# A decoder kernel whose logarithm and exponential share one table load, and whose weight blocks come in two transfers each

## What is computed

```python
def stick_breaking_attention(q, k, v):          # A[t,s] = beta[t,s] * prod_{s<j<t} (1 - beta[t,j])
    ...
    mask = s_idx < t_idx
    log_keep = jnp.where(mask, jax.nn.log_sigmoid(-logits), 0.0)
    later = lax.cumsum(log_keep, axis=log_keep.ndim - 1, reverse=True) - log_keep
    log_a = jax.nn.log_sigmoid(logits) + later
    a = jnp.where(mask, jnp.exp(log_a), 0.0)
    ...

def s5_mixer(h, ...):
    ...
    g = jax.nn.gelu(y).astype(h.dtype)
    val, gate = jnp.split(g @ w_glu, 2, axis=-1)
    return val * jax.nn.sigmoid(gate)
```

## Time and profile before

| | us |
|---|---|
| median of 3 runs | 1056.37 (1052.62 to 1057.84) |
| the profiled execution | 1056.6 |
| its span, from the first to the last instruction | 1054.8 |
| PE busy | 931.1 (88%) |
| DVE busy | 574.7 (54%) |
| ACT busy | 461.0 (44%) |
| POOL busy | 125.4 (12%) |
| DMA | 163.93 MB, mean 155 GB/s |

### The profile page before, as it was taken

How to read it: one execution, slowest core, us unless ns; L and a number is a source line. 1 busy time by engine, 2 the same in 40 slices (tenths; PEclk the granted TensorE clock), 3 DMA queues, 4 the chain that set the end, 5 groups by cost and what they waited for, 6 DMA issues and landing times.

```text
span 1054.8 us, 11941 instructions
## 1 busy us (share of the span) xinstructions
PE 931.1 (88%) x4951; PEld 766.0 (73%) x4951; DVE 574.7 (54%) x751; ACT 461.0 (44%) x568; POOL 125.4 (12%) x71
## 2 busy tenths in 40 slices
PE   4999999989999999897699999984445999999998
PEld 3887777777787886786588888774335877888886
DVE  4654555561244766666576899632620555545453
ACT  4534555458934636244244444422212544444441
POOL 1000002020000020202844444000002000000000
PEclk9999999996999998698899999995765999999999
DMA  8525644441014554004447566643997454455441
GB/s 322 184 88 192 239 160 160 163 156 42 1 68 156 165 199 163 3 2 160 149 165 255 201 230 217 218 162 40 102 149 278 140 211 157 162 185 214 160 160 40
DMA packets 72736, 163.93 MB, mean 155 GB/s; under 512 B 2041, under 2 KB 12874, under 8 KB 72170
## 3 DMA queue, kind: packets, MB, share of 16 engines
q1 hardware_dynamic: 68304, 149.03, 43.4%
q10 hardware_dynamic: 2234, 6.69, 2.1%
q0 software_dynamic: 2144, 7.43, 2.0%
HBM read 150.57 MB, written 11.53 MB: 154 GB/s over the span
## 4 chain that ended last, share of the span: by engine, by line
PE 42%; DVE 6%; DMA 3%; SPq 3%; ACT 2%; issue 1%; POOL 0%; POOLq 0%; ACTq 0%
PE bank L560 13%; PE bank L562 12%; PE bank L561 12%; DVE wlo L1333 3%; SPq L506 3%; DMA ring<-in_w_glu 2%; PE bank L814 1%; DMA aux<-h 1%; ACT whi L1003 1%; DMA ring<-scratch_readout 1%; PE bank L553 1%; DVE aux L1726 1%; PE bank L925 1%; PE bank L895 1%; PE bank L859 0%
## 5 line engine op out<-in xcount | busy, mean ns | idle before, releaser
L1333 DVE TENSOR_TENSOR wlo<-ring,whi 128x2048 fp32r<-128x2048 f32 (+1 forms) x122 | 307.5, 2528 | 248.3 <-ACT whi L1003 248.3
L1003 ACT ACTIVATE whi<-ring 128x2048 fp32r<-128x2048 f32 (+1 forms) x124 | 236.2, 1910 | 343.9 <-PE bank L562 241.3
L560 PE MATMUL bank<-whi,hT_hi 128*128 128x512 f32 (+1 forms) x736 | 292.4, 397 | 21.8 <-DVE hT_lo L1324 10.3
L561 PE MATMUL bank<-wlo,hT_hi 128*128 128x512 f32 (+1 forms) x736 | 289.7, 394 | 0.0
L562 PE MATMUL bank<-whi,hT_lo 128*128 128x512 f32 (+1 forms) x736 | 289.4, 393 | 0.0
L560 PEld LDWEIGHTS bank<-whi,hT_hi 128*128 128x128 f32 x736 | 140.5, 191 | 52.1 <-DVE hT_lo L1324 8.7
L562 PEld LDWEIGHTS bank<-whi,hT_lo 128*128 128x128 f32 x736 | 140.5, 191 | 29.1
L561 PEld LDWEIGHTS bank<-wlo,hT_hi 128*128 128x128 f32 x736 | 140.6, 191 | 28.1
L560 PE MATMUL bank<-whi,hidT_hi 128*128 128x512 f32 x256 | 100.7, 393 | 2.1 <-DVE hidT_lo L1719 2.1
L562 PE MATMUL bank<-whi,hidT_lo 128*128 128x512 f32 x256 | 99.8, 390 | 0.0
L561 PE MATMUL bank<-wlo,hidT_hi 128*128 128x512 f32 x256 | 99.6, 389 | 0.0
(11 more groups left out here) (232 smaller groups left out, 1044.2 us busy)
## 6 DMA issues: line engine op xcount, KB each, us to landing
ring<-in_w_ff SPq DMA_DIRECT2D x32, 2048.0 KB, 7.7
ring<-in_ple_gate_w SPq DMA_DIRECT2D x4, 2048.0 KB, 7.9
ring<-in_w_kv SPq DMA_DIRECT2D x4, 2048.0 KB, 8.0
ring<-in_b_w_in SPq DMA_DIRECT2D x4, 2048.0 KB, 8.5
ring<-in_w_glu SPq DMA_DIRECT2D x4, 2048.0 KB, 9.0
ring<-in_a_w_in SPq DMA_DIRECT2D x3, 2048.0 KB, 9.2
ring<-in_w_in SPq DMA_DIRECT2D x3, 2048.0 KB, 8.1
ring<-in_a_w_out SPq DMA_DIRECT2D x2, 2048.0 KB, 8.0
```

What stands on the lines that cost most here:

```text
L560: pe.matmul(bank_cols, high[:, at[0], at[1]], w_high, start=first, stop=False)
L561: pe.matmul(bank_cols, high[:, at[0], at[1]], w_low, start=False, stop=False)
L1003: act.activation(whi[at], ring[:, slot[name], cols], ACT.Copy).then_inc(high_made, 1)
L1333: dve.tensor_tensor(wlo[at], ring[:, slot[name], cols], whi[at], ALU.subtract).then_inc(low_made, 1)
```

## The change

It has two parts.

1. ACT loads a set by name, `natural_log_exp_and_others`, ahead of the stick-breaking loop, and finds both functions in it.
2. Every split block comes in two transfers of half a block, each with a semaphore of its own (`block_landed[slot][half]`), and ACT's `fill(g)` waits for its own half alone. SP waits ahead of each half: for the first, that the first half of the low part of block n - 2 is made (both halves where the two blocks differ in size), for the second, that both are. Where block n - 2 isn't a split one, both halves wait for its product, as before. Blocks that aren't split come in whole.

```diff
+    landed, arrived = {}, [[0, 0] for _ in range(RING)]
+    for name, parts, _ in blocks:
+        counts = arrived[slot[name]]
+        for half in range(2 if name in order else 1):
+            counts[half] += 16 if name in order else 16 * len(parts)
+            landed[name, half] = counts[half]
...
-        block_landed = [sem(f"block_landed{i}") for i in range(RING)]
+        block_landed = [[sem(f"block_landed{i}{half}") for half in "ab"] for i in range(RING)]
...
+                if name in order:
+
+                    (_, src), = parts
+                    k, width = src.shape[1] // 2, src.shape[2]
+                    for half in range(2):
+                        if n >= RING:
+                            before, _, reader = blocks[n - RING]
+                            if before in order:
+                                whole = size[before] != size[name] or half
+                                sp.wait_ge(low_made, 2 * order[before] + (2 if whole else 1))
+                            else:
+                                sp.wait_ge(pe_done, done(reader))
+                        dst = ring[:, slot[name], half * k * width:(half + 1) * k * width]
+                        sp.dma_start(dst.rearrange("p (k n) -> p k n", k=k), src[:, half * k:(half + 1) * k])\
+                            .then_inc(block_landed[slot[name]][half], 16)
+                    continue
...
             def fill(g):
 
                 name, cols, at = half_of(g)
-                if g:
-                    act.wait_ge(block_landed[slot[name]], landed[name])
-                else:
-                    act.wait_ge(first_landed, 16)
+                act.wait_ge(block_landed[slot[name]][g % 2], landed[name, g % 2])
...
             turned_out("q", [(qT, "q_norm", True)])
+            act.preload_act_table_set("natural_log_exp_and_others")
             for j in range(NH // 2 + 1):
```

More of the change, by code:

```diff
@@ L319, in program @@
     slot = {name: n % RING for n, (name, _, _) in enumerate(blocks)}
[L320 to L323, removed]
     done = u.done
@@ L399, in program @@
                                                       for n in ("inject", "readout", "taps"))
-        high_made, low_made, high_turned, inv_ready, gelu_high, relu_ready, first_used, exps_ready, first_landed = (
+        high_made, low_made, high_turned, inv_ready, gelu_high, relu_ready, first_used, exps_ready = (
             sem(n) for n in ("high_made", "low_made", "high_turned", "inv_ready", "gelu_high", "relu_ready",
-                             "first_used", "exps_ready", "first_landed"))
+                             "first_used", "exps_ready"))
         def half_of(g):
@@ L477, in _ @@
             sp.dma_start(ring[:, 0, 0:BLK // 2].rearrange("p (k n) -> p k n", k=KC // 2), first[:, 0:KC // 2])\
-                .then_inc(first_landed, 16)
+                .then_inc(block_landed[0][0], 16)
             sp.wait_ge(x_landed, 16)
             sp.dma_start(ring[:, 0, BLK // 2:BLK].rearrange("p (k n) -> p k n", k=KC // 2), first[:, KC // 2:KC])\
-                .then_inc(block_landed[0], 16)
+                .then_inc(block_landed[0][1], 16)
             for n, (name, parts, _) in enumerate(blocks):
@@ L506, in _ @@
                         sp.dma_start(ring[GI * j:GI * j + GI, slot[name], :].rearrange("p (g n) -> p g n", n=P), src)\
-                            .then_inc(block_landed[slot[name]], 16)
+                            .then_inc(block_landed[slot[name]][0], 16)
                     continue
@@ L513, in _ @@
                         dst = dst.rearrange("p (k n) -> p k n", k=src.shape[1])
-                    sp.dma_start(dst, src).then_inc(block_landed[slot[name]], 16)
+                    sp.dma_start(dst, src).then_inc(block_landed[slot[name]][0], 16)
             for t in range(NT):
@@ L540, in weights_here @@
             def weights_here(name):
-                pe.wait_ge(block_landed[slot[name]], landed[name])
+                pe.wait_ge(block_landed[slot[name]][0], landed[name, 0])
             def turn(stage, src, units=range(4), width=P, chunks=8, ready=None):
```

## The result

| | before | after |
|---|---|---|
| median, us | 1056.97 (1052.62 to 1057.84) | 1036.41 (1035.9 to 1044.95) |
| profiled execution, us | 1056.6 | 1036.74 |
| span, us | 1054.8 | 1034.9 |
| PE busy, us | 931.1 | 919.7 |
| ACT busy, us | 461.0 | 443.1 |

The ratio is 0.9839 (95% interval 0.9805 to 0.9872), a gain of 20.6 us between the medians. The 14 runs of the three sets go from 1035.2 to 1045.0 us with a median of 1039.0, so the gain is nearer to 18 than to 21 us. Both medians, 1036.4 and 1039.0, lie outside the forecast range. The forecast was 1046.2 us with a range of 1041 to 1051.5: right in sign and too small. All medians and ranges are of runs in the fast state; one run of `tables` took 1374.06 us at a mean clock of 0.642, where its others had 0.93, and is left out.

The account below looks back on a forecast made before the run. PE was taken to bound the large-product stages, leaving gains only in the stick-breaking loop, bound by PE once ACT's loads go, and the S5 stage. 7.1 + 2.7 + 0.6 = 10.4 us off 1056.6 gives 1046.2 us, range 1041 to 1051.5.

Parts of the forecast that it names:

- loop, low stretch as long as before: Stick-breaking loop: one table load gains 7.1 us, from 3.8 of PE's waits, 3.2 of low-clock spells and 0.1.
- PE's waits for low parts: Between 300 and 345: PE's one wait for a low part, 0.6 us, should go.
- `readout` 1: S5 stage: it is issued and lands 2.7 us earlier, cutting PE's wait from 3.2 to 0.5 us; gain 2.7.
- the first stretch at the low clock: Loop's start, 20.48 us long: the change doesn't touch the wait ahead, PE bounds already, only 0.1 us gained.
- The only rival on the clock that I priced for that stretch: Loop: low clock stays, each further step costs 4.5 us, 1077 us with all six; chance of three or more 0.04.
- it waits only before the last sums: Loop's last step, which has no logits: about 0.5 us of PE's wait stays; elsewhere the round trip is hidden.
- the spells of 3.4 us: Loop: two low-clock spells, at 279.02 and 292.67, go with the waits preceding them; gain 3.2 us.
- The step was forecast at 5.43 us: Loop: each step is cut from 6.15 to at most 5.43 us, the 0.72 that PE waits for `sps`.
- the first rival: Loop: the clock dips all the same, so the total gain is 7.2 us and the time 1049.4; chance 0.2.
- The rival in which PE isn't the bound: Loop: PE's busy time hides slack, saving 15 us there at the most, time 1038; chance 0.05.
- land apart and in order: S5 stage: the first half of ("val", 0) lands 2.7 us ahead of the whole block, bounds 2.3 and 3.3.
- 27 us of PE's waits for the taps: S5 stage: PE's 27 us of waiting for the taps don't change, as they come in ahead of the block.

Follow-up runs that it names:

- the three sets: The changed kernel timed three times, unaltered, the second and third beside other kernels on their chips: ratios 0.9839, 0.9835 and 0.9843 to the kernel before.
- tables: The kernel before with the one table load alone, transfers whole: 1045.82 us, ratio 0.9901.
- val0_dve: The changed kernel with the two low parts of block ("val", 0) made by VectorE in place of GpSimd: 1037.42 us, ratio 0.9816.
- again: The changed kernel once more, unaltered: 1038.59 us, ratio 0.9835.
- again_2: The changed kernel a third time, unaltered: 1040.49 us, ratio 0.9843.
- tables_again: The kernel before with the one table load alone, once more on another chip: 1045.86 us, ratio 0.9898.
- act_extra: The changed kernel with an unread 128x512 copy on ACT behind each final exponential, 16 in the loop: 1040.64 us, ratio 0.9854.
- filled_before: The kernel before with seven unused 128x512 products on PE in its wait for the turned q ahead of the loop: 1058.56 us, ratio 1.0007.
- halves: The changed kernel without the table line, so half transfers alone: 1050.69 us, ratio 0.9939.
- val0_only: The changed kernel with only block ("val", 0) and the very first split block in halves, all others whole: 1043.9 us, ratio 0.9883.
- filled4_dve: The changed kernel with four unused products in PE's wait ahead of the loop and ("val", 0)'s low parts on VectorE: 1034.12 us, ratio 0.9795.

## Why the prediction was wrong in size

The forecast gain was 10.4 us: 7.1 for the loop, 2.7 for the S5 stage and 0.6 near 342. The two profiles differ by 19.9 us, 9.5 more. Of these, 6.0 are in the loop (13.1 against 7.1), 2.2 ahead of it, 0.3 between loop and S5 stage, and 1.0 in the S5 stage. Term by term:

| term | forecast | shown |
|---|---|---|
| loop, low stretch as long as before | 7.1 | 8.6 (`tables`, `val0_dve`) |
| loop, the stretch shorter | 0 | 4.5 (after, `again`, `again_2`) |
| PE's waits for low parts | 0.6 | 0.7 near 122 and 0.9 near 342 |
| `readout` 1 | 2.7 | about 1.4, of which 1.0 is its own wait and 0.4 that for `readout` 0 |

**The step that failed** is the one on the first stretch at the low clock: in it "PE bounds already, and next to nothing (0.1 us) is gained". That took its 20.48 us as given, like a piece of the code. It isn't: `tables` and `tables_again` are the same code and had 20.5 and 10.2 us; after, `again`, `again_2` and `act_extra` had 10.2, and `val0_dve`, whose code up to there is theirs, 20.5. With the long one the loop takes 51.20 us, with the short one 46.66: each microsecond at the low clock costs 0.44 us, since PE now bounds. Without any stretch it takes 42.57, 8.6 us less than with the long one; in the kernel before, with ACT as the bound, the same removal gave 2.9 us (`filled_before`, with one short spell more). The only rival on the clock that I priced for that stretch was that it lasts longer, 4.5 us per step. The same price should have stood on the other side of the forecast: one step less gives 1041.7, and two give 1037. With this term at 4.5 instead of 0.1 the forecast would have been 1041.8. Of the eight profiled loops with one table load and no fillers six had 10.2 us and two 20.5, so the shorter one is the more frequent there; why can't be told from these traces. The one run of before that was profiled had 20.48, and whether its other runs do is open. For that reason the 4.5 us are shown between profiles only; that the medians of the runs lie apart by it isn't shown.

**The rest of the loop was sized too small**, by 1.5 us. 0.9 of them are the stretch that in `tables` began 1.05 us ahead of the first logits, 0.15 ahead in before; the remainder lies behind the stretch. The mechanism held: PE is the bound, it waits only before the last sums (0.30 us, forecast 0.5), and the spells of 3.4 us went with the waits. The step was forecast at 5.43 us, the 6.15 less the wait of 0.72. The end of the last logits, from which that wait is counted, is hidden where the sums follow at once: they then start 2.04 us behind the first logits, not 2.19, and the step is 5.23. Of the first rival (the clock dips all the same), nothing was seen: no profile with the one table load has a dip behind the first stretch. The rival in which PE isn't the bound had a time (1038) close to the result, but that is luck, not its mechanism: `act_extra` keeps ACT busy for 7.5 us more, and the loop grows by 0.8.

On the Trainium skill's price for a switch of table sets (ScalarE: Activation LUTs, What ACT_TABLE_LOAD costs), 2.66 us with a drain: ACT was busy for 50.36 us in the loop of `halves` and 30.14 in that of `tables`, a difference of 20.2 us for 17 loads, or 1.2 us for each; a drain of 1.38 us isn't in it, nor is it idle time, of which ACT's loads had 0.1 us in front of them. The measurement decides for 1.28 us.

**The halves.** That they land apart and in order was right: 2.60 us apart, forecast 2.7. The halves of `("val", 0)` bring the issue of `readout` 1 from 11.0 us behind the block's last byte (before, `tables`, `tables_again`, `filled_before`) to 8.4 (the eight halved kernels with GpSimd): 2.6 us, as forecast. What was wrong is that all of this would reach PE. The transfer of `readout` 1 takes 7.3 to 7.7 us in those four and 8.3 to 9.0 in those eight, and PE's wait for it falls only from 3.4 on the mean to 2.4; another 0.4 us comes from `readout` 0, which PE gets earlier in the seven with all blocks in halves (a wait of 7.4 us; 7.9 in `val0_only`). The prediction let a transfer start earlier and keep its length. Its 27 us of PE's waits for the taps were also misread, 15.58 + 13.47 = 29.1 in before; no term uses them. It named only one wait of PE for a low part and missed the one at 122, which it had not looked for.

The stage shows the same when the taps, which scatter by 8.6 us, are taken out of it (us; the taps from their first issue to their last landing):

| | S5 stage less taps | mean |
|---|---|---|
| the four with whole blocks | 50.6 to 51.9 | 51.3 |
| the eight with halves, low parts on GpSimd | 49.3 to 50.5 | 49.8 |
| the two with low parts on VectorE | 46.3 and 47.2 | 46.7 |

So the halves alone are worth 1.5 us here, and the faster engine behind them another 3.0.

**What belongs to chance.** Of the 19.9 us between the two profiles, about 1.6 are a low spell at 186.9 in before that is absent in after, and also in `tables` and `halves`, and some 2.2 are the taps, whose transfers took 42.95 us in before and 40.71 in after. In the other kernels, which issue the same taps, they took from 39.1 to 47.7 us. The attributable terms (loop, the two waits for low parts, the S5 stage) come to 8.6 + 1.6 + 1.4 = 11.6 us with the long stretch and 16.1 with the short one. The measured gain of 18 us is a little more than that, and the 2 us between aren't assigned.

**The range.** It held the sides of the mechanisms that I had named, but 2 us of spread for the runs was too little: the runs of the kernel before alone go from 1051.4 to 1062.4 on one chip. The bound of the range at 1041 was also drawn without any case below it but one of 0.05.

## What to carry to other kernels

When an edit makes another engine the bound, first price what that engine's own changing state costs, in both directions: here 10 us more or less at TensorE's low clock became worth 4.5 us as soon as PE bounded. Functions that alternate in a loop should come from one table set, and what that is worth is read from the waits of the engine behind it, not from the loads removed (20.2 us off ACT gave 8.6 to 14.3). A transfer that is issued earlier moves next to another one: ask for its length there, and look whether a faster engine can free the slot.

## What the runs showed of the hardware

- The stretch at the low clock at the start of this loop lasted 10.2, 13.7 or 20.5 us, with PE busy for 93% of it and more, and in the same code both 10.2 and 20.5. Seven or four products in the 3.4 us wait ahead of it (three profiles of the changed kernel and `filled_before`) removed it; in `filled_before` a spell of 3.4 us came 7.5 us into the loop. The Trainium skill (TensorE: Matmul & The Clock Gate, Part 1) says that the number of slow matmuls at a kernel's start differs from run to run of the same kernel, and the traces show the like at this later place: 31 to 34 matmuls in the short ones, 66 to 69 in the long ones. Where the clock fell 1.05 us ahead of the first logits the stretch was long (`tables`, `val0_dve`), at 0.8 us ahead it was 13.7 us (`halves`), and at 0.6 us ahead or later short, with before (0.15 ahead, 20.48 us) as the exception; these are too few to make a rule.
- In the kernels with table loads in the loop, the spells of 3.4 us came at other places each time (279.0 and 292.7 in before, 269.0 in `halves`, 248.2, 278.9 and 292.5 in `filled_before`), each worth about 1.7 us.
- A `readout` block of 2 MB takes 7.3 to 7.7 us when issued 1.4 us or more behind the landing of the one ahead of it, and 8.3 to 9.0 when issued within 0.8 us of it, on either side. Issued 4.1 us before that landing it took 10.61 us, and the two together 13.8 (`val0_dve`); issued 2.8 us before it, 9.04 and 13.4 (`filled4_dve`). Whether it is the nearness or the halves around it that makes it longer wasn't separated.
- Exponentials and logarithms cost the same from the shared set as from the two: 523 and 514 ns before, 523 and 512 ns after.
